# Weight products that read their moving operand as two halves in turns

## The reference

```python
# first block
h = rmsnorm(x, pre_mix_g); proj = h @ w_in          # q, k, v of three attentions, three gates
ya, yb, yc = diff_attention(...), sliding_window_attention(...), moba_attention(...)
mix = ga * (ya @ w_oa) + gb * (yb @ w_ob) + gc * (yc @ w_oc)
x = x + rmsnorm(mix @ w_out, post_mix_g)
h = rmsnorm(x, pre_ffn_g)
x = x + rmsnorm(conv_ffn(h, w_up, conv_w, conv_b, w_down), post_ffn_g)   # 2048 -> 11264 -> 5632 -> 2048
# second block: 16 meta tokens in front of x, then two layers
h = h + rmsnorm(attention_mixer(rmsnorm(h), attn_w_in, ..., attn_w_out))
h = h + rmsnorm(gla_mixer(rmsnorm(h), gla_w_in, ..., gla_w_out))
return h[:, 16:]
```

## Time and profile before

| | |
|---|---|
| median of 3 runs | 2269.96 us (2269.36 to 2270.67) |
| span of the profiled execution | 2267.8 us |
| PE busy | 2243.5 us, 99% |
| DVE busy | 1448.2 us, 64% |
| ACT busy | 1197.3 us, 53% |
| POOL busy | 192.3 us, 8% |
| DMA | 405.69 MB, mean 179 GB/s |
| mean granted clock of TensorE | 0.998 |

### The profile page before, as it was taken

One profiled execution on the slowest core, in us unless ns is written; L12 is line 12 of the kernel. 1 busy time (PEld: TensorE's weight loads), 2 busy tenths in 40 slices (PEclk: granted clock), 3 DMA queues, 4 the chain that ended last, 5 costly groups with the idle time before them and its releaser, 6 DMA issues.

```text
span 2267.8 us, 43774 instructions
## 1 busy us (share of the span) xinstructions
PE 2243.5 (99%) x17103; PEld 2126.7 (94%) x17103; DVE 1448.2 (64%) x1913; ACT 1197.3 (53%) x1813; POOL 192.3 (8%) x146
## 2 busy tenths in 40 slices
PE   9999999999999999999999999999999999999998
PEld 8898999999889999999988889999999999999986
DVE  5556644458567777777754556998666465566754
ACT  5455644445454545545544445445666565676553
POOL 0000000000002212122100000221000000012110
PEclk9999999999999999999999999999999999999999
DMA  8645566657646566665666665555335547554453
GB/s 287 184 145 158 155 197 192 191 165 237 198 151 200 180 206 189 188 202 178 208 197 192 192 194 157 188 188 172 112 119 172 176 137 220 166 150 140 140 195 139
DMA packets 258873, 405.69 MB, mean 179 GB/s; under 512 B 16655, under 2 KB 115852, under 8 KB 257708
## 3 DMA queue, kind: packets, MB, share of 16 engines
q1 hardware_dynamic: 257060, 396.87, 56.6%
q10 hardware_dynamic: 1688, 7.07, 0.9%
HBM read 396.32 MB, written 4.22 MB: 177 GB/s over the span
## 4 chain that ended last, share of the span: by engine, by line
PE 95%; DVE 2%; ACT 1%; DMA 1%; issue 0%; SPq 0%; DVEq 0%; ACTq 0%
PE bank L2214 67%; PE bank L2319 14%; PE bank L2787 4%; PE bank L2229 2%; PE bank L2533 1%; PE bank L2755 1%; PE bank L2711 1%; PE bank L2571 1%; PE bank L2505 0%; DVE xtok L1521 0%; PE bank L2254 0%; PE bank L2542 0%; DMA xtok<-in_x 0%; PE bank L2513 0%; PE bank L2703 0%
## 5 line engine op out<-in xcount | busy, mean ns | idle before, releaser
L1372 DVE TENSOR_TENSOR wlo<-raw,whi 128x1024 fp32r<-128x1024 f32 (+1 forms) x748 | 927.7, 1250 | 660.1 <-ACT whi L676 656.9
L2214 PE MATMUL bank<-ahi,whi 128*128 128x256 f32 (+1 forms) x4224 | 1196.0, 283 | 5.7 <-DVE alo L1586 3.7
L2214 PE MATMUL bank<-ahi,wlo 128*128 128x256 f32 (+1 forms) x4224 | 1181.4, 280 | 0.0
L2214 PE MATMUL bank<-alo,whi 128*128 128x256 f32 (+1 forms) x4224 | 1181.3, 280 | 0.0
L676 ACT ACTIVATE whi<-raw 128x1024 fp32r<-128x1024 f32 (+1 forms) x748 | 774.4, 1040 | 690.2 <-PE bank L2214 460.5
L2214 PEld LDWEIGHTS bank<-ahi,whi 128*128 128x128 f32 x4224 | 794.1, 188 | 13.1 <-issue 8.1
L2214 PEld LDWEIGHTS bank<-alo,whi 128*128 128x128 f32 x4224 | 794.4, 188 | 1.4 <-issue 0.2
L2214 PEld LDWEIGHTS bank<-ahi,wlo 128*128 128x128 f32 x4224 | 793.8, 188 | 0.0
L2319 PE MATMUL bank<-whi,ghi 128*128 128x512 f32 x352 | 137.0, 389 | 0.0
L2319 PE MATMUL bank<-wlo,ghi 128*128 128x512 f32 x352 | 136.9, 389 | 0.0
L2319 PE MATMUL bank<-whi,glo 128*128 128x512 f32 x352 | 136.9, 389 | 0.0
(11 more groups left out here) (388 smaller groups left out, 2232.7 us busy)
## 6 DMA issues: line engine op xcount, KB each, us to landing
raw<-in_w_up SPq DMA_DIRECT2D x176, 512.0 KB, 4.6
raw<-in_w_in SPq DMA_DIRECT2D x156, 512.0 KB, 4.1
raw<-in_attn_w_in SPq DMA_DIRECT2D x96, 512.0 KB, 4.2
raw<-in_gla_w_in SPq DMA_DIRECT2D x96, 512.0 KB, 3.8
raw<-in_w_down SPq DMA_DIRECT2D x80, 512.0 KB, 4.4
raw<-in_w_out SPq DMA_DIRECT2D x32, 512.0 KB, 4.4
raw<-in_attn_w_out SPq DMA_DIRECT2D x32, 512.0 KB, 3.7
raw<-in_gla_w_out SPq DMA_DIRECT2D x32, 512.0 KB, 4.2
```

What stands on the lines that cost most here:

```text
L1372: dve.tensor_tensor(wlo[:, u % RING, 0:c], raw[:, u % RAW, 0:c], whi[:, u % RING, 0:c].bitcast(F32), ALU.subtract).then_inc(wlo_ready, 1)
L2214: mm = pe.matmul(bank[:, base + t, 0:T], w[wp][:, k, col:col + P], rhs(ap, k0 + k), start=begins and k == 0 and (wp, ap) == (0, 0), stop=e ...
```

## The change

The moving operand of lines 2214, 2229, 2319, 2440 and 2787 is no longer read in the order 0, 1, 2, ... but as two halves in turns: 0, N/2, 1, N/2+1, and so on, for N = 256, 272, 512 or 128. The same floats are read, and the same number of matmuls is issued. The columns of the PSUM tile then stand in that order. So everybody who takes such a tile out reads the even columns first and the odd columns after them, which is a step of two floats in PSUM, and writes (and reads its other operand) in two contiguous halves. The scaling in `up` no longer works in place: it reads columns 0 to 255 with a step of two and writes columns 256 to 511 of the same bank in the right order, and the convolution reads those. The stationary operands, the small products and the DMAs stay.

```diff
+        def in_turns(ap):
+            return ap.rearrange("p (h c) -> p c h", h=2)
+        def halves(ap):
+            return ap.rearrange("p (h c) -> p h c", h=2)
+        def untwined(ap):
+            return ap.rearrange("p (c h) -> p h c", h=2)
+        def halves_of(ap):
+            return ap.rearrange("p k (h c) -> p k h c", h=2)
+        def untwined_of(ap):
+            return ap.rearrange("p k (c h) -> p k h c", h=2)
...
-                            mm = pe.matmul(bank[:, base + t, 0:T], w[wp][:, k, col:col + P], rhs(ap, k0 + k),
+                            mm = pe.matmul(bank[:, base + t, 0:T], w[wp][:, k, col:col + P], in_turns(rhs(ap, k0 + k)),
...
-                                           w[wp][:, k, cols[0]:cols[1]],
+                                           in_turns(w[wp][:, k, cols[0]:cols[1]]),
...
-                            mm = pe.matmul(bank[:, row_bank(b, c, tt), :], tokens_of, w[wp][:, k, :],
+                            mm = pe.matmul(bank[:, row_bank(b, c, tt), :], tokens_of, in_turns(w[wp][:, k, :]),
...
-                        mm = pe.matmul(bank[:, 0, 0:TB], w[wp][:, k, 0:P], ha((ahi, alo)[ap], k0 + k, 0, TB),
+                        mm = pe.matmul(bank[:, 0, 0:TB], w[wp][:, k, 0:P], in_turns(ha((ahi, alo)[ap], k0 + k, 0, TB)),
...
-                                mm = pe.matmul(bank[:, b, :], gated(ap, k0 + k)[:, tt * P:(tt + 1) * P], w[wp][:, k, :],
+                                mm = pe.matmul(bank[:, b, :], gated(ap, k0 + k)[:, tt * P:(tt + 1) * P], in_turns(w[wp][:, k, :]),
...
-                        act.activation(dst_of(i, chunk, t), bank[:, t, 0:T], func).then_inc(acc_free, 1)
+                        act.activation(halves(dst_of(i, chunk, t)), untwined(bank[:, t, 0:T]), func).then_inc(acc_free, 1)
...
-                act.activation(cv[:, t, :], bank[:, 4 * chunk + t, 0:TB], ACT.Identity,
+                act.activation(cv[:, t, :], bank[:, 4 * chunk + t, TB:2 * TB], ACT.Identity,
...
-                dve.tensor_tensor(mixtmp[:, min(branch, 1), :, :], bank[:, b:b + 4, 0:TB], gate[:, k:k + 4, :], ALU.mult)\
+                dve.tensor_tensor(halves_of(mixtmp[:, min(branch, 1), :, :]), untwined_of(bank[:, b:b + 4, 0:TB]),
+                                  halves_of(gate[:, k:k + 4, :]), ALU.mult)\
...
-                    rows = bank[:, 4 * chunk + t, 0:TB]
-                    dve.tensor_tensor(rows, rows, rxrow[:, 0:TB], ALU.mult).then_inc(up_scaled, 1)
+                    summed, scaled = bank[:, 4 * chunk + t, 0:TB], bank[:, 4 * chunk + t, TB:2 * TB]
+                    dve.tensor_tensor(halves(scaled), untwined(summed), halves(rxrow[:, 0:TB]), ALU.mult).then_inc(up_scaled, 1)
```

More of the change, by code:

```diff
@@ L971, in read_out @@
                             passed(u, t + 1, i, n)
-                            act.activation((q, k)[chunk][:, t, :], bank[:, t, 0:TB], ACT.Copy).then_inc(acc_free, 1)
+                            act.activation(halves((q, k)[chunk][:, t, :]), untwined(bank[:, t, 0:TB]), ACT.Copy).then_inc(acc_free, 1)
                     else:
@@ L975, in read_out @@
                             passed(u, (1, 4)[tt], i, n)
-                            act.activation(v[:, tt, :], bank[:, tt, :], ACT.Copy).then_inc(acc_free, (1, 3)[tt])
+                            act.activation(halves(v[:, tt, :]), untwined(bank[:, tt, :]), ACT.Copy).then_inc(acc_free, (1, 3)[tt])
                 return read_out
@@ L985, in kvb_out @@
                 passed(u, 1, i, n)
-                act.activation(kbT[:, 0, :], bank[:, 0, 0:TB], ACT.Copy)
-                act.activation(kbT[0:64, 1, :], bank[64:128, 0, 0:TB], ACT.Copy)
-                act.activation(kbT[64:128, 1, :], bank[0:64, 0, 0:TB], ACT.Copy).then_inc(acc_free, 1)
+                act.activation(halves(kbT[:, 0, :]), untwined(bank[:, 0, 0:TB]), ACT.Copy)
+                act.activation(halves(kbT[0:64, 1, :]), untwined(bank[64:128, 0, 0:TB]), ACT.Copy)
+                act.activation(halves(kbT[64:128, 1, :]), untwined(bank[0:64, 0, 0:TB]), ACT.Copy).then_inc(acc_free, 1)
                 for tt in range(2):
                     passed(u, (2, 4)[tt], i, n)
-                    ins = act.activation(vbtok[:, tt, :], bank[:, 1 + tt, 0:P], ACT.Copy)
+                    ins = act.activation(halves(vbtok[:, tt, :]), untwined(bank[:, 1 + tt, 0:P]), ACT.Copy)
                     ins.then_inc(acc_free, (1, 2)[tt])
@@ L1002, in gates_out @@
                     passed(u, t + 1, i, n)
-                    act.activation(gate[:, bass.ds(i * 4 + t, 1), :], bank[:, t:t + 1, 0:TB], ACT.Sigmoid,
+                    act.activation(halves_of(gate[:, bass.ds(i * 4 + t, 1), :]), untwined_of(bank[:, t:t + 1, 0:TB]), ACT.Sigmoid,
                                    bias=par[:, bass.ds(i * 4 + (PAR["b_gate"] + t), 1)]).then_inc(acc_free, 1)
@@ L1076, in read_out @@
                         passed(u, t + 1, i, n)
-                        act.activation(dst[:, bass.ds(i * 4 + t, 1), 0:T], bank[:, t:t + 1, 0:T], func, scale=scale)\
+                        act.activation(halves_of(dst[:, bass.ds(i * 4 + t, 1), 0:T]), untwined_of(bank[:, t:t + 1, 0:T]), func, scale=scale)\
                            .then_inc(acc_free, 1)
@@ L1461, in rows_gained @@
                 dve.wait_ge(y_squared, 8 * (b - 1) + 2 * c + tt + 1)
-                y = dve.tensor_tensor(y_rows(b, tt, 512 * c, 512), bank[:, row_bank(b, c, tt), :].rearrange("p (k f) -> p k f", f=P),
-                                      gain_rows(b, 512 * c, 512), ALU.mult)
+                rows, made, gain = bank[:, row_bank(b, c, tt), :], y_rows(b, tt, 512 * c, 512), gain_rows(b, 512 * c, 512)
+                if b == 3:
+                    y = dve.tensor_tensor(made, rows.rearrange("p (k f) -> p k f", f=P), gain, ALU.mult)
+                else:
+                    by_half = "p (h k) f -> p h k f"
+                    y = dve.tensor_tensor(made.rearrange(by_half, h=2), rows.rearrange("p (k f h) -> p h k f", h=2, f=P),
+                                          gain.rearrange(by_half, h=2), ALU.mult)
                 if b == 3:
@@ L1792, in up_out @@
                         tap = par[:, bass.ds(i * 4 + (PAR["conv_w"] + (2 - back) * 2 * FT + r), 1)]
-                        dve.scalar_tensor_tensor(cv[:, t, back:TB], bank[:, 4 * chunk + t, 0:TB - back], tap,
+                        dve.scalar_tensor_tensor(cv[:, t, back:TB], bank[:, 4 * chunk + t, TB:2 * TB - back], tap,
                                                  cv[:, t, back:TB], ALU.mult, ALU.add).then_inc((tap1, acc_free)[back - 1], 1)
@@ L2153, in rows_out @@
                     c = 512 * (2 * i + chunk)
-                    dve.tensor_tensor(yrow[:, tt, c:c + 512], bank[:, 2 * chunk + tt, :], gainrow[:, c:c + 512], ALU.mult)\
+                    dve.tensor_tensor(halves(yrow[:, tt, c:c + 512]), untwined(bank[:, 2 * chunk + tt, :]), halves(gainrow[:, c:c + 512]),
+                                      ALU.mult)\
                        .then_inc(y_gained, 1)
```

## The result

The changed kernel takes 2203.25 us (median of 4 runs, 2201.75 to 2203.54) against 2269.66 us in the same session: a ratio of 0.9706, 95% interval 0.9692 to 0.972, or 66.4 us less. The forecast was 7836 us. Even the sign was wrong; rival D, to which I gave 3 in 100, had the direction.

A forecast was written before the change was run, and what follows sets the result against it. The prediction took PE (TensorE), open for 99% of the span, to bound the kernel. It added 5566 us for reading in turns and 0 for the other parts to 2270, giving 7836 us; range 4030 to 8310 for 8 in 10.

The forecast's parts named there:

- rival D: Large PE products: reading in turns avoids an extra cycle per 16 neighbouring floats, 134 us saved, 2136 us; chance 0.03.
- The bound: Whole kernel: PE is fed throughout, so each nanosecond that a product takes longer is paid in full.
- part 1: Moving operand of the large PE products read in turns: each lone float costs 1.66 ns, adding 5566 us.
- Parts 2 and 3: ACT and DVE reading PSUM with step two: 0, up to 15 us; scaling in `up` out of place: 0.
- A: Large PE products: half rate, one float per cycle of 1.2 GHz, 4059 us; chance 0.30.
- C: Large PE products: rate unchanged by the order, 2270 us, to 2285 with PSUM's step in the open; chance 0.14.
- the two rivals near 2270: Large PE products: C, no change in rate, 2270 us, chance 0.14; rival D, faster, 2136 us, chance 0.03.

The follow-up runs named there:

- `m_idle`: No model: 26 stretches of 144 fp32r products, only moving operand, start or held columns differing, other engines quiet; 512 columns contiguous 233.3 ns, halves in turns 215.8.
- `m_lanes`: No model, quiet chip: stretches of 144 products in further read orders and plain float32, then DVE and ACT reads; each half stepping two 233.3 ns, stepping four 453.3.
- `only_272`: Only the 4224 products with 272 columns read in turns, PSUM readers contiguous, against the kernel before: 2242.64 us, ratio 0.9882.
- `m_busy`: Same stretches as `m_idle`, with ACT copying, DVE subtracting and DMAs landing meanwhile; 512 columns contiguous 233.3 ns, in turns 215.8.

## Why the prediction was wrong

**The bound, right.** PE set the end, and nearly each nanosecond of a product was paid or saved: the distances times the counts (9264 x 1.7 + 4224 x 7.6 + 1056 x 10.7 + 384 x 13.1 + 384 x 12.8 + 192 x 12.9 ns) give 71.5 us, of which 66.4 arrived. In the profiled executions PE's time without work grew by 4.0 us (from 2267.8 - 2243.5 to 2201.7 - 2173.4), and the two stretches at half clock cost some 3 us more; the distances, taken from single stretches, are not exact enough to close that sum.

**The failed step** is in part 1: "SBUF hands out one 16-byte piece per about 1.67 ns to a reader, and a reader that takes only one float of it waits for the next." The price of a lone float is right for DVE and for ACT, both measured, and for a plain float32 product if it reads its operand once per record. Wrong was to count PE as one reader, and to judge the order by what lies between successive floats of the stream. An fp32r product behaves as two readers that take every second float each. Reading halves in turns does not scatter a run: it turns two readers that each step by two floats into two readers that each run along a contiguous half. So the term that I put at +5566 us was -71.5, of which 66.4 reached the median. I should have been warned by my own numbers: at one column per 2.4 GHz cycle PE took floats twice as fast as any other reader in the trace, which one reader like the others could not do. I also took the plain products of the earlier trace rows for half as fast as fp32r ones. Their four records are two `matmul`s of line 2755, so a plain product takes 430 ns against 113.4, nearly four times as long.

**The rule on lines.** The Trainium skill, "SBUF — State Buffer", box on cachelines in "Door 1: The DMA port swizzle", asks for two hits on a 16-byte line for full bandwidth. The trace agrees in the main if the hits in a row are counted for each lane: four hits 215.8 ns, two hits 227.0 to 233.4 (252.2 for fours in turns), one hit 433 to 462. So two hits are nearly enough here, not quite. Counted along the stream, as I did, it speaks against a change that it in fact favours.

**Parts 2 and 3, right.** The step of two in PSUM and the scaling out of place cost nothing that a run shows: 470, 424 and 1220 ns stayed.

**The rivals.** A (half rate, 4059 us) is what lone floats cost, 433 ns for 512, but the change leaves no lane with lone floats. C (nothing) was off by 3%. D was right that the overhead of contiguous reading is a price that the change takes away, and wrong in the mechanism (neighbours: floats read twice or overlapping are neighbours too and cost 215.9) and in the size, 134 us: 2.5 ns per product stay, and 256 columns have a floor. That floor is the weight load: in turns, 256 columns take 16.08 / 144 = 111.7 ns with 128 columns held and 15.72 / 144 = 109.2 with 32 held, in these stretches of `m_idle`:

```profile
713.85 16.08 PE bank L176 x144
...
746.73 15.72 PE bank L182 x144
```

and in `m_lanes` 128 columns take 111.3 to 111.7 ns, no less than 256. D counted on 6.7 ns for each of the 9264 products of 256 columns and there were 1.7: 46 of the 62 us between its 134 and the 71.5.

**The range** ended at 4030 us, because I left the two rivals near 2270, 0.17 in sum, outside it. The evidence for that was one row of another engine.

**Open.** That PE has two fetching paths is inferred from times; the runs exclude one reader with a price per jump, one reader that holds several pieces, the tested traffic of other engines, and (at 512 columns) the weight load as the main cause, but no record names the paths. Why a lane that alternates between two pieces pays 1.05 ns per float (plain float32 in turns), 283.3 / 256 = 1.11 (quarters) or 327.1 / 256 = 1.28 (pairs) and not 1.68, which hints at a piece that is kept, and why a contiguous start address is worth up to 6 ns in 233, was not settled. The held operand has a part in the last: moved by 128 bytes, with the moving one where it was, it gave 32.97 / 144 = 229.0 ns (line 222 of `m_lanes`) instead of 233.3. And 256 contiguous columns took longer with 32 columns held (16.80 / 144 = 116.7 ns in `m_idle`) than with 128 (16.32 / 144 = 113.3), which the floor does not explain.

## What to carry to other kernels

For fp32r products look at every second float of the moving operand: the best order gives each of the two a contiguous run (0, N/2, 1, N/2 + 1, ...), which buys 5 to 8% over contiguous for 272 or more columns and almost nothing for 256 with 128 columns held, where the weight load is the floor; the readers of PSUM could undo it with a step of two at no measured price. Never give either of the two lone floats: that doubles the product, and pairs in turns already cost 40%. Before carrying a price from one engine to another, ask how many such readers the other engine must have to reach the rate that it shows.

## What the runs showed of the hardware

- fp32r products, 512 columns: 215.8 ns in turns, 227.0 to 233.4 contiguous (forwards, backwards, or in two runs, by start address), 433 to 462 with lone floats; not moved by 0.1 ns by ACT and DVE at 97% and DMA at 395 GB/s.
- Plain float32 products leave two records for a call, each at 0.84 ns per column, so one `matmul` takes 3.7 times as long as a contiguous fp32r one (858 against 233 ns for 512 columns), and in turns is worse for them (540.0 against 429.2 a record).
- A lone float out of SBUF (step of 16) costs 1.68 ns in a record of a plain product, 1.71 on DVE and 1.74 on ACT. The last two are the price of a contiguous float, (1226 - 692) / 512 = 1.04 and (1061 - 630) / 512 = 0.84, from the 1024 floats of `m_busy` (1226 and 1061 ns) and the 512 of `m_lanes`, plus the 0.67 and 0.90 of the step. So three engines come within 4% of each other. From PSUM, a step of two floats cost ACT and DVE nothing (470 and 471 ns, 1220 and 1220).
- The granted clock of TensorE fell to 1.2 GHz in the middle of a run, behind pauses of PE: twice in the changed kernel's profile, three times in that of `only_272`, never in that of the kernel before. Each time cost some 1.5 us (products of 272 columns every 227 ns instead of every 116).
